# An opening in eight chunks of 256 channels instead of four of 512

## The chip, the cores and the metric

## What is computed

The kernel is one decoder layer on 256 tokens of 2048 channels. Only its beginning matters here:

```python
mod = c_act @ w_ada[l] + b_ada[l]                 # (2048,) @ (2048, 12288)
sh1, sc1, gt1, sh2, sc2, gt2 = split(mod, 6)
h = x * (1.0 + sc1) + sh1                         # x: 256 x 2048
proj = h @ w_in[l]
xr, gr, q_c, kv_c, k_r, g_rnn, g_mla = split(proj)
...   # recurrent branch, attention, output projection, norm, expert layer, norm
```

No row of `proj` can be finished before all 2048 channels of `h` are there, and a channel of `h` needs its column of `sh1` and of `sc1`, that is a sum over all 2048 rows of `w_ada`. The opening therefore reads the first 4096 columns of `w_ada` (32 MB), sums them on DVE, and multiplies the channels of `h` that are ready with the rows of `w_in` that belong to them.

## The kernel before

**Layout.** Channels lie on the 128 partitions in 16 tiles of 128 (`KT`), so `hT` is 16 tiles of 128 x 256 tokens. `x` is loaded transposed into the place of `hT` and changed there. `ring` is four slots of 1 MB (2048 words on each partition).

**The opening** goes over four chunks `j` of 512 channels (four tiles of `hT`). For each chunk:

1. SP (function `ada`, L378) loads eight ring slots of `ada_first`. One slot holds two of the 16 row tiles `kt`, each 1024 wide (512 columns of shift and 512 of scale). A slot is loaded again as soon as DVE has used both of its row tiles (semaphore `ada_used`). Behind the chunk's slots SP issues the early weights: a unit of 1 MB for each of three projections (`B_QC`, `B_KVC`, `B_XR`, L395) and half a unit (L398). In chunk 0 it also loads `xT` (2 MB, L389) and `w_kr` (1 MB, L400).
2. DVE adds the 16 row tiles up: one TENSOR_SCALAR (L1480) and 15 SCALAR_TENSOR_TENSOR (L1478), each 128x1024, each waiting for the one before by semaphore, since they all write the same sum. The sum is still spread over partitions.
3. PE (`ada_columns`) multiplies the sum, in eight pieces of 128 columns, by a column of ones. Each piece gives one column of shift or scale.
4. DVE adds the bias (L1486, L1487) and changes four tiles of `hT` by L1491 (semaphore `hT_ok`).
5. PE multiplies: `early_unit` three times (four tiles deep, four matmuls each), `w_kr` (four matmuls), then `ada_columns` of the next chunk, then `early_half` (eight matmuls). PE works in this order and cannot take the later one first.

Between the chunks DVE does small work that other parts need: `softplus()` after chunk 0 (L1412 to L1436), `angles()` after chunk 1 (L1441 to L1458), `sines()` after chunk 2. ACT answers with an exponential and two sines.

**Behind the opening** ACT copies the latents out of PSUM (L1059), `krraw` (L1064), the recurrent input (L1068) and its gate (L1072, which waits for the last `early_half`), DVE squares the latents, and PE goes on with norms, queries and the loop over heads. Weights for that loop are requested when the latents are normed, and POOL's loads of the rest of `w_ada` start after `rope_ok`.

Of the kernel before, what the change touches and what calls it, by code (L numbers as in the profile page):

```python
# [12 lines left out]
ALU = mybir.AluOpType  # L13
# [30 lines left out]
B_QC, B_KVC, B_XR, B_G, B_G2, B_RNN, B_MLA, B_O, B_WQ, B_END = 0, 1, 2, 10, 12, 18, 22, 26, 30, 34  # L44
ADA_UNITS = 2 * KT
SLOT_BASE = ADA_UNITS // RING - B_XR
B_SPLIT = B_XR + 2
# [42 lines left out]
def layouts(a):  # L90

    w_in, w_ada = a["w_in"][0], a["w_ada"][0]
    first = w_ada[:, :2 * D].reshape(2, RING, 2, P, 2, 4, 512).transpose(5, 0, 1, 3, 2, 4, 6)
    uq = a["w_uq"][0].reshape(LT, P, HEADS, NOPE + ROPE)
# [52 lines left out]
def build(nc, t, out):  # L147
    with ExitStack() as ctx:
        def sem(name):
            return ctx.enter_context(nc.semaphore(name))  # L150
# [16 lines left out]
        def at(off, n):  # L167
            return arena[:, off:off + n]
# [9 lines left out]
        def small(n):  # L178
            sm[0] += n
            assert sm[0] <= ARENA  # L180
            return sm[0] - n
# [5 lines left out]
        hT = at3(R_HT, KT, S)  # L187
        acc = at(R_G + KT * S, 2 * D).rearrange("p (j h c) -> p j h c", j=4, h=2)

# [14 lines left out]
        cact = at(small(16), 16)  # L204
        sh1 = at(small(4), 4)
        sc1 = at(small(4), 4)
        sp4 = at(small(16), 16)
# [112 lines left out]

        in_cst, in_par, in_pos, in_xT, in_kr = (sem(n) for n in ("in_cst", "in_par", "in_pos", "in_xT", "in_kr"))
        in_ring = [sem(f"in_ring{i}") for i in range(RING)]
        in_head = [sem(f"in_head{i}") for i in range(2)]
# [5 lines left out]
        in_early = [sem(f"in_early{i}") for i in range(6)]  # L329
        halves_used = sem("halves_used")  # L330
        in_ada = [sem(f"in_ada{i}") for i in range(3)]
# [39 lines left out]
        def _(sp):  # L371
            sp.dma_start(at(o_par, P + 24 + 6 * KT), t["par"]).then_inc(in_par, 16)

            def ada(j, i, first):
                for s in range(RING):
                    if not first:
                        sp.wait_ge(ada_used, i * 8 + (16 * j + 2 * (s - 3)))
                    sp.dma_start(ring[s], t["ada_first"][bass.ds(i * (RING * P) + (8 * j + s) * P, P), :]).then_inc(in_ring[s], 16)  # L378

# [5 lines left out]

            for j in range(4):
                if j == 0:
                    ada(0, 0, True)
                    sp.dma_start(at(R_HT, KT * S), t["xT"]).then_inc(in_xT, 16)  # L389
                with sp.Fori(1 if j == 0 else 0, 2) as i:  # L390
                    ada(j, i, False)
                for c, b in enumerate((B_QC, B_KVC, B_XR)):
                    if j >= 2:
                        sp.wait_ge(unit_used, 3 * j - 5 + c)
                    sp.dma_start(early_flat[3 * (j % 2) + c], input_unit(b, j)).then_inc(in_early[3 * (j % 2) + c], 16)  # L395
                if j >= 2:
                    sp.wait_ge(halves_used, j - 1)
                sp.dma_start(half_flat[j % 2], half_unit(0, j)).then_inc(in_head[j % 2], 16)  # L398
                if j == 0:
                    sp.dma_start(at(R_OT, KT * 2 * ROPE), t["w_kr"]).then_inc(in_kr, 16)  # L400

            def units(w, g, b):
# [5 lines left out]
            sp.dma_start(at(R_G, LT * HEADS * ROPE), t["w_uqr"]).then_inc(in_uqr, 16)  # L408
            sp.wait_ge(ada_used, 2 * ADA_UNITS)
            for s in range(RING):  # L410
# [56 lines left out]
            query_weights(9, in_wq[9])  # L467
            sp.wait_ge(modc_done, 12)
            query_weights(10, in_wq[10])
# [135 lines left out]
        def _(pe):  # L605
# [17 lines left out]
            def early_half(j):  # L623

                pe.wait_ge(in_head[j % 2], 16 * (j // 2 + 1))
                for k in range(4):
                    kt = 4 * j + k
                    for m in range(2):
                        last = mm(ps[:, 5, m * S:(m + 1) * S], half_w[j % 2][:, k, m * P:(m + 1) * P], hT[:, kt, :], kt == 0 and m == 0, kt == KT - 1)
                last.then_inc(halves_used, 1)  # L630

            def ada_columns(j):

                pe.wait_ge(acc_ok, j + 1)
                for h in range(2):
                    for k in range(4):
                        o = S + 8 * j + 4 * h + k
                        last = mm(ps[:, 4, o:o + 1], acc[:, j, h, k * P:(k + 1) * P], ones[:, 0:1], j == 0 and h == 0 and k == 0, True)
                last.then_inc(modc_done, 1)

            def early_unit(j, c):

                o = ps[:, (6, 2, 0)[c]:(6, 2, 0)[c] + 2, :].rearrange("p b (h c) -> p (b h) c", h=2)
                i = 3 * (j % 2) + c
                pe.wait_ge(in_early[i], 16 * (j // 2 + 1))
                for k in range(4):
                    kt = 4 * j + k
                    for m in range(4):
                        last = mm(o[:, m, :], early_w[i][:, k, m * P:(m + 1) * P], hT[:, kt, :], kt == 0 and m % 2 == 0, kt == KT - 1)
                last.then_inc(unit_used, 1)  # L650

            ada_columns(0)
            for j in range(4):
                pe.wait_ge(hT_ok, 4 * j + 4)
                for c in range(3 if j < 3 else 2):
                    early_unit(j, c)
                pe.wait_ge(in_kr, 16)
                for kt in range(4 * j, 4 * j + 4):
                    last = mm(ps[:, 4, 0:S], krw[:, kt, :], hT[:, kt, :], False, kt == KT - 1)
                if j < 3:  # L660
                    ada_columns(j + 1)
                    early_half(j)
            last.then_inc(kr_done, 1)
            early_unit(3, 2)
            early_half(3)
            pe.wait_ge(kr_out, 1)
# [28 lines left out]
            def queries(h):  # L695
                b = h % 2
                pe.wait_ge(in_head[b], 32 * (h // 2 + 2))
                if h and h % 4 == 0:
# [344 lines left out]
        def _(act):  # L1043
# [6 lines left out]
            A(sigc, colB[:, 0:16], ACT.Sigmoid).then_inc(sigc_ok, 1)  # L1050
            act.wait_ge(y_need, 1)
            A(lt[1], lt[0], ACT.Exp, scale=-1.0).then_inc(y_ok, 1)
            act.wait_ge(r_ok, 1)
            A(pt[3], pt[2], ACT.Sin).then_inc(sin_ok, 1)
            A(pt[4], pt[2], ACT.Sin, scale=0.5).then_inc(sin_ok, 1)

            def latent(b, off, bank):
# [12 lines left out]
            channels_out(B_XR, infront(XR, 1024))  # L1070
            act.wait_ge(halves_used, 4)
            A(infront(GR, 512), ps[:, 5, :], ACT.Copy)  # L1072
# [325 lines left out]
        def _(dve):  # L1398
# [69 lines left out]

            for j in range(4):
                part = at(R_G + KT * S + 1024 * j, 1024)  # L1470
                for kt in range(KT):
                    i, s = kt // 8, kt // 2 % RING
                    if kt % 2 == 0:
                        dve.wait_ge(in_ring[s], j * 32 + 16 * (i + 1))
                    raw = ring[s][:, kt % 2 * 1024:(kt % 2 + 1) * 1024]
                    if kt:
                        dve.wait_ge(ada_used, j * KT + kt)
                        STT(part, raw, cact[:, kt:kt + 1], part, ALU.mult, ALU.add).then_inc(ada_used, 1)  # L1478
                    else:
                        TS(part, raw, cact[:, 0:1], None, ALU.mult).then_inc(ada_used, 1)  # L1480
                dve.wait_ge(ada_used, j * KT + KT)
                dve.sem_inc(acc_ok, 1)

                dve.wait_ge(modc_done, j + 1)
                dve.wait_ge(in_xT, 16)
                me.do(TT(sh1, ps[:, 4, S + 8 * j:S + 8 * j + 4], modc[:, 4 * j:4 * j + 4], ALU.add))  # L1486
                me.do(TT(sc1, ps[:, 4, S + 8 * j + 4:S + 8 * j + 8], modc[:, KT + 4 * j:KT + 4 * j + 4], ALU.add))  # L1487
                me.wait()
                for k in range(4):
                    h = at(R_HT + 1024 * j + S * k, S)  # L1490
                    TS(h, h, sc1[:, k:k + 1], sh1[:, k:k + 1], ALU.mult, ALU.add).then_inc(hT_ok, 1)  # L1491
                if j == 0:
                    softplus()
                if j == 1:
                    angles()
                if j == 2:
                    sines()

            for i, lat in enumerate((qcT, kvT)):
# [104 lines left out]
            def columns(n, count):  # L1604
                dve.wait_ge(modc_done, 4 + n + count)
                c = modc[:, 2 * KT + 8 * n:2 * KT + 8 * (n + count)]
                TT(c, c, ps[:, 4, 0:8 * count], ALU.add).then_inc(col_ok, 1)
# [471 lines left out]
```

## Time and profile before

| | us |
|---|---|
| median of 3 runs | 2320.36 (2319.26 to 2324.15) |
| the profiled execution | 2321.49 |
| its span, first to last instruction | 2319.5 |
| PE busy / DVE busy in the span | 2058.7 (89%) / 1483.0 (64%) |
| bytes read | 805.10 MB |

All times of rows are counted from the start of the span. A timeline row gives start, length, engine, line, operation and how many of them it merges, with the idle time ahead of it and what ended that. The chain of work that ended last is followed back from the last instruction. A windows row gives the busy time of each engine in a stretch, with the clock granted to TensorE as a share of full speed, the busy share of the DMA engines and what they moved.

### The profile page before, as it was taken

How to read it: one execution, taken by the hardware profiler on the slowest of the kernel's cores; microseconds unless marked ns; L12 is line 12 of the kernel's file. 1: busy time of each engine (PE TensorE's matmuls, PEld its weight loads, DVE VectorE, ACT ScalarE, POOL GpSimd, SP SyncE). 2: the span in 40 equal slices, each digit the busy share in tenths (PEclk: the TensorE clock that was granted, in tenths of full speed). 3: DMA queues.
4: the chain of work that ended last, by engine and by line, in shares of the span. 5: the costliest groups of instructions: out<-in, count | busy, mean ns of one | idle time of the engine just before them, and what ended most of it. 6: DMA issues, size and time to landing. Idle time of an engine off the chain costs nothing.

```text
span 2319.5 us, 23058 instructions
## 1 busy us (share of the span) xinstructions
PE 2058.7 (89%) x7678; PEld 1334.9 (58%) x7678; DVE 1483.0 (64%) x2119; ACT 573.3 (25%) x1103; POOL 763.3 (33%) x764
## 2 busy tenths in 40 slices
PE   3999999999999999999987888787878788888977
PEld 3888999977888887787433333333333333333333
DVE  6837866967876556688366656664666668465444
ACT  0014455453343333322111101111111111112011
POOL 0001010101211000056465554555555454445562
PEclk9999999999999999999999888988898998889999
DMA  9946676657988664689899999999999999999996
GB/s 394 421 199 243 228 272 216 242 210 280 385 315 284 224 219 163 254 354 406 362 422 421 422 422 422 422 422 421 422 421 422 422 421 421 422 421 417 420 423 263
DMA packets 125637, 808.30 MB, mean 348 GB/s; under 512 B 14068, under 2 KB 14452, under 8 KB 38132
## 3 DMA queue, kind: packets, MB, share of 16 engines
q0 software_dynamic: 92160, 604.02, 63.9%
q1 hardware_dynamic: 33112, 202.70, 23.4%
q8 instruction: 51, 0.84, 0.1%
q10 hardware_dynamic: 288, 0.53, 0.1%
q14 instruction: 26, 0.21, 0.0%
HBM read 805.10 MB, written 2.10 MB: 348 GB/s over the span
## 4 chain that ended last, share of the span: by engine, by line
PE 53%; DMA 22%; DVE 8%; POOL 7%; issue 6%; ACT 4%; POOLq 0%; ACTq 0%; DVEq 0%; SPq 0%
PE ps L607 52%; DMA front<-in_peer_u,arena 17%; DVE front L1977 3%; DMA front<-in_ada_first 2%; POOL arena L548 2%; POOL front L540 1%; POOL arena L540 1%; POOL arena L528 1%; DMA front<-in_peer_v,arena 1%; DMA arena<-in_peer_v,arena 1%; DMA arena<-in_w_ada 1%; DVE arena L1478 1%; POOL front L548 1%; POOL front L594 0%; DVE split_ring L1631 0%
## 5 line engine op out<-in xcount | busy, mean ns | idle before, releaser
L607 PE MATMUL ps<-arena 128*128 128x512 f32 (+5 forms) x2798 | 962.4, 497 | 237.5 <-ACT arena L1297 186.9
L607 PEld LDWEIGHTS ps<-arena 128*128 128x128 f32 (+1 forms) x2798 | 512.7, 206 | 669.3 <-issue 486.0
L1977 DVE CUSTOM_DVE_ANT_0 front<-front,arena 128x2048 f32<-128x2048 f32 x180 | 410.0, 2293 | 201.2 <-DMA front<-in_peer_u,arena 195.0
L607 PE MATMUL ps<-front,arena 128*128 128x512 f32 (+1 forms) x832 | 355.9, 576 | 2.2 <-DMA front<-in_peer_v,arena 2.2
L1977 DVE CUSTOM_DVE_ANT_0 arena<-arena 128x2048 f32<-128x2048 f32 x60 | 137.4, 2294 | 265.6 <-DMA arena<-in_peer_u,arena 264.7
L607 PEld LDWEIGHTS ps<-front,arena 128*128 128x128 f32 x832 | 157.3, 190 | 191.3 <-issue 186.0
L540 POOL DMA_INDIRECT front<-in_peer_u,arena x176 | 239.0, 1358 | 68.4 <-issue 44.9
L1285 ACT ACTIVATE arena<-arena 128x4 f32<-128x4 f32 x64 | 13.2, 207 | 906.9 <-DVE arena L1957 906.7
L1631 DVE TENSOR_TENSOR split_ring<-front,split_pada 128x2048 fp32r<-128x2048 f32 x72 | 164.9, 2291 | 110.5 <-ACT split_pada L1180 110.1
L528 POOL COPY arena<-arena 128x4 uint32 (+1 forms) x120 | 85.8, 715 | 377.7 <-PE ps L607 356.9
L1180 ACT ACTIVATE split_pada<-front 128x2048 fp32r<-128x2048 f32 x70 | 134.1, 1916 | 234.4 <-PE ps L607 234.4
L499 POOL DMA_DIRECT2D arena<-in_w_ada x64 | 34.0, 532 | 474.3 <-DVEq L1543 189.2
L548 POOL DMA_INDIRECT arena<-in_peer_v,arena x153 | 162.1, 1060 | 77.7 <-POOL arena L528 48.6
L607 PE MATMUL ps<-arena,front 128*128 128x256 f32 (+2 forms) x864 | 173.0, 360 | 0.6 <-ACT arena L1311 0.6
L607 PEld LDWEIGHTS ps<-arena,front 128*128 128x128 f32 x864 | 152.6, 195 | 18.9 <-ACT arena L1311 0.8
L607 PE MATMUL ps<-split_pada,split_ht 128*128 128x512 f32 x320 | 125.8, 393 | 0.0
L607 PE MATMUL ps<-split_f,split_ring 128*128 128x256 f32 x384 | 108.6, 283 | 0.0
L504 POOL DMA_DIRECT2D arena<-in_w_ada x64 | 33.8, 528 | 210.8 <-DVE front L1727 103.6
L607 PE MATMUL ps<-split_pada,split_w 128*128 128x512 f32 x256 | 101.3, 396 | 1.8 <-DVE split_ring L1631 1.8
L607 PE MATMUL ps<-split_ring,split_f 128*128 128x512 f32 x256 | 101.3, 396 | 0.0
L607 PE MATMUL ps<-split_ring,split_w 128*128 128x512 f32 x256 | 100.4, 392 | 0.0
L548 POOL DMA_INDIRECT front<-in_peer_v,arena x91 | 90.0, 989 | 29.3 <-issue 29.3
(254 smaller groups left out, 2561.2 us busy)
## 6 DMA issues: line engine op xcount, KB each, us to landing
front<-in_w_in_u SPq DMA_DIRECT2D x64, 1024.0 KB, 6.8
arena<-in_w_ada POOLq DMA_DIRECT2D x128, 512.0 KB, 6.4
front<-in_ada_first SPq DMA_DIRECT2D x32, 1024.0 KB, 11.8
front<-in_w_rnn_out_u SPq DMA_DIRECT2D x16, 1024.0 KB, 6.3
front<-in_w_mla_out_u SPq DMA_DIRECT2D x16, 1024.0 KB, 4.9
front<-in_w_o_u SPq DMA_DIRECT2D x16, 1024.0 KB, 4.8
front<-in_peer_wq_u SPq DMA_DIRECT2D x11, 1024.0 KB, 8.8
arena<-in_w_ukv_h SPq DMA_DIRECT2D x16, 512.0 KB, 5.5
```

The costliest lines, as they stand in the source:

```text
L499: pool.dma_start(ada_raw[i % 3], ada_v[:, i % KT:i % KT + 1, 2 * D + 1024 * (i // KT):2 * D + 1024 * (i // KT + 1)].rearrange("p t c -> p ...
L504: pool.dma_start(ada_raw2[kt % 4], ada_v[:, kt:kt + 1, bass.ds(n * 1024 + 4 * D, 1024)].rearrange("p t c -> p (t c)")).then_inc(in_ada2[kt ...
L528: me.do(pool.tensor_copy(ix[:, e % 8:e % 8 + GROUP], arena[:, bass.ds(H * TOPK + (o_idx + e), GROUP)].bitcast(U32)))
L540: pool.indirect_dma_start(uslot[s], None, t["peer_u"][0], bass.IndirectOffsetOnAxis(idxu[:, s:s + 1], 0)).then_inc(in_u[s], 16)
L548: pool.indirect_dma_start(vslot[s], None, t["peer_v"][0], bass.IndirectOffsetOnAxis(idxv[:, s:s + 1], 0)).then_inc(in_v[s], 16)
L607: return pe.matmul(o, l, r, start=start, stop=stop, skip_group_check=True, **k)
L1180: A(whi[s % 2], ring[s], ACT.Copy).then_inc(whi_ok, 1)
L1285: me.do(A(zs[:, c0:c1], zu[:, c0:c1], ACT.Sigmoid, scale=GELU_S))
L1478: STT(part, raw, cact[:, kt:kt + 1], part, ALU.mult, ALU.add).then_inc(ada_used, 1)
L1631: TT(wlo[s], ring[s], whi[s % 2].bitcast(F32), ALU.subtract).then_inc(wlo_ok, 1)
L1977: V.tensor_tensor_reduce(uslot[s], uslot[s], h2[T], 1.0, 0.0, ALU.mult, ALU.add, zraw[:, s:s + 1]).then_inc(dots_done, 1)
```

## The change

The opening runs over `CHUNKS = 8` chunks of 256 channels (two tiles of `hT`). A ring slot still has 1 MB but now holds four row tiles, each 512 wide (256 of shift, 256 of scale), so a chunk takes four slots. DVE's sums are 128x512 and twice as many. `ada_columns` takes four pieces for a chunk, `hT` is changed two tiles at a time. The early weights come in half units: each of the old transfers is two of half the bytes, and `early_unit`, `early_half` and the `w_kr` products run two tiles deep. Of `xT` the first two tiles come ahead of the early weights (0.25 MB) and the other 14 behind `w_kr`. `softplus()` is now after chunk 5, `sines()` after chunk 3, `angles()` stays after chunk 1; ACT does the sines before the exponential.

```diff
-                    sp.dma_start(ring[s], t["ada_first"][bass.ds(i * (RING * P) + (8 * j + s) * P, P), :]).then_inc(in_ring[s], 16)
+                    if j:
+                        sp.wait_ge(ada_used, KT * (j - 1) + 4 * (s + 1))
+                    sp.dma_start(ring[s], t["ada_first"][(RING * j + s) * P:(RING * j + s + 1) * P, :]).then_inc(in_ring[s], 16)
...
+            for j in range(CHUNKS):
+                u, k = j // 2, j % 2
+                ada(j)
                 if j == 0:
-                    ada(0, 0, True)
-                    sp.dma_start(at(R_HT, KT * S), t["xT"]).then_inc(in_xT, 16)
-                with sp.Fori(1 if j == 0 else 0, 2) as i:
-                    ada(j, i, False)
+                    sp.dma_start(at(R_HT, 2 * S), t["xT"][:, 0:2 * S]).then_inc(in_xT0, 16)
...
+                    i, before = 3 * (u % 2) + c, 2 * (u // 2) + k
+                    if before:
+                        sp.wait_ge(in_early[i], 16 * before)
+                    sp.dma_start(early_flat[i][:, 1024 * k:1024 * (k + 1)], input_unit(b, u)[:, 1024 * k:1024 * (k + 1)]).then_inc(in_early[i], 16)
...
                 if j == 0:
                     sp.dma_start(at(R_OT, KT * 2 * ROPE), t["w_kr"]).then_inc(in_kr, 16)
+                    sp.dma_start(at(R_HT + 2 * S, (KT - 2) * S), t["xT"][:, 2 * S:]).then_inc(in_xT, 16)
...
-            for j in range(4):
-                part = at(R_G + KT * S + 1024 * j, 1024)
+            for j in range(CHUNKS):
+                part = at(R_G + KT * S + 512 * j, 512)
                 for kt in range(KT):
-                    i, s = kt // 8, kt // 2 % RING
-                    if kt % 2 == 0:
-                        dve.wait_ge(in_ring[s], j * 32 + 16 * (i + 1))
-                    raw = ring[s][:, kt % 2 * 1024:(kt % 2 + 1) * 1024]
+                    s = kt // 4
+                    if kt % 4 == 0:
+                        dve.wait_ge(in_ring[s], 16 * (j + 1))
+                    raw = ring[s][:, kt % 4 * 512:(kt % 4 + 1) * 512]
...
-                for k in range(4):
-                    h = at(R_HT + 1024 * j + S * k, S)
+                for k in range(2):
+                    h = at(R_HT + 512 * j + S * k, S)
                     TS(h, h, sc1[:, k:k + 1], sh1[:, k:k + 1], ALU.mult, ALU.add).then_inc(hT_ok, 1)
-                if j == 0:
-                    softplus()
                 if j == 1:
                     angles()
-                if j == 2:
+                if j == 3:
                     sines()
+                if j == 5:
+                    softplus()
```

## Rows read from the trace of the kernel before

**Rows 1.** The chain of work that ended last, stretch 0 to 260 us: start us, us, what.
```profile
10.76 12.66 DMA front<-in_ada_first
...
23.45 1.30 DVE arena L1478
...
24.77 1.30 DVE arena L1478
...
26.16 1.29 DVE arena L1478
...
66.64 150.79 PE ps L607 x754
```

**Rows 2.** Windows: length, busy time by engine, PEclk, DMA share, GB/s.
```profile
8.70:128.00 119.30, 89.09 (x412) 78.88 (x413) 92.36 (x116) 2.22 (x4) 0.00 (x0) 0.97 1.01 422
128.00:157.00 29.00, 29.00 (x136) 25.51 (x136) 3.35 (x5) 3.74 (x5) 0.00 (x0) 1.00 0.33 136
```

**Rows 3.** Timeline of the opening, SP's issues and the first sum.
```profile
8.66 0.75 DVE L1480 TENSOR_SCALAR arena<-front,arena 128x1024 f32<-128x1024 f32 x1 [3.58 <-DMA front<-in_ada_first]
...
10.76 8.72 SPq L378 DMA_DIRECT2D front<-in_ada_first  x4
```

**Rows 4.** Timeline, DVE: what stands between two chunks.
```profile
37.96 0.16 DVE L1486 TENSOR_TENSOR arena<-ps,arena 128x4 f32<-128x4 f32 x1 [3.79 <-PE ps L607]
...
38.23 1.38 DVE L1491 TENSOR_SCALAR arena<-arena 128x256 f32<-128x256 f32 x4
39.53 0.17 DVE L1412 TENSOR_SCALAR arena<-arena 128x16 f32<-128x16 f32 x1
...
43.55 0.18 DVE L1436 TENSOR_SCALAR arena<-arena 128x16 f32<-128x16 f32 x1
...
70.25 0.16 DVE L1486 TENSOR_TENSOR arena<-ps,arena 128x4 f32<-128x4 f32 x1 [3.72 <-PE ps L607]
...
75.01 0.75 DVE L1480 TENSOR_SCALAR arena<-front,arena 128x1024 f32<-128x1024 f32 x1 [0.16 <-DVE arena L1458]
75.80 20.30 DVE L1478 SCALAR_TENSOR_TENSOR arena<-front,arena 128x1024 f32<-128x1024 f32 x15
```

**Rows 5.** Timeline, PE: columns of a chunk (128x1) and the products (128x256).
```profile
34.38 3.55 PE L607 MATMUL ps<-arena 128*128 128x1 f32 x16 [34.38 <-DVEq L1482]
...
116.74 7.07 PE L607 MATMUL ps<-arena,front 128*128 128x256 f32 x32
```

**Rows 6.** Windows around the columns of chunks 1 and 3.
```profile
38.00:39.60 1.60, 0.00 (x0) 0.00 (x0) 1.56 (x7) 0.00 (x0) 0.00 (x0) 1.00 1.07 435
...
63.80:66.10 2.30, 0.05 (x1) 0.00 (x0) 2.16 (x3) 0.00 (x0) 0.00 (x0) 1.00 0.98 410
66.10:72.90 6.80, 6.26 (x23) 5.72 (x24) 2.93 (x11) 0.00 (x0) 0.00 (x0) 0.53 1.02 422
...
125.40:127.20 1.80, 1.80 (x18) 1.80 (x17) 0.00 (x0) 0.00 (x0) 0.00 (x0) 1.00 1.07 441
```

**Rows 7.** Groups by line and form, DVE: count, busy us, mean ns, idle before.
```profile
L1478 DVE SCALAR_TENSOR_TENSOR arena<-front,arena 128x1024 f32<-128x1024 f32 x60 | 77.1, 1284 | 9.7 <-DMA front<-in_ada_first 6.1
...
L1987 DVE SCALAR_TENSOR_TENSOR arena<-arena 128x512 f32<-128x512 f32 x8 | 6.0, 748 | 0.1
...
L1513 DVE SCALAR_TENSOR_TENSOR arena<-arena 128x256 f32<-128x256 f32 x8 | 3.3, 481 | 0.1
...
L1864 DVE TENSOR_SCALAR arena<-arena 128x512 f32<-128x512 f32 x4 | 1.9, 546 | 0.0
```

**Rows 8.** Timeline, the end of the opening.
```profile
127.25 0.16 DVE L1486 TENSOR_TENSOR arena<-ps,arena 128x4 f32<-128x4 f32 x1 [2.54 <-PE ps L607]
...
156.72 0.60 ACT L1072 ACTIVATE front<-ps 128x512 f32<-128x512 f32 x1 [2.43 <-PE ps L607]
```

**Rows 9.** DMA issues, whole span: count, KB each, median us from issue to landing.
```profile
front<-in_w_mla_out_u SPq DMA_DIRECT2D x16, 1024.0 KB, 4.9
...
arena<-in_w_uq_h SPq DMA_DIRECT2D x16, 256.0 KB, 3.3
```

## What the change does to the time, and why

> **What bounds the kernel now.** I read the chain of work that ended last first, because it says which engine the opening waits for. Up to 66.6 us it alternates between transfers of `ada_first` and DVE's sums; from 66.64 us it is PE without a gap for 150.8 us [rows 1]. So the kernel ends when PE's row of work ends, and two things about PE matter: when it can start, and how much stands behind the last sum. The windows say the same: between 8.7 and 128 us the DMA engines are full at 422 GB/s, PE is busy 89.1 of 119.3 us and DVE 92.4; between 128 and 157 us PE is busy for all 29 us and hardly anything else runs [rows 2]. PE's first instruction is at 34.38 us [rows 5], since the first sum needs 8 MB.
>
> The marker for everything below is ACT's copy at 156.72 us, which waits for the last product of the opening [rows 8]. What follows has no clock of its own: the head loop's weights wait for the normed latents, and POOL's loads wait for the ropes. Hence I let a shift of the marker pass to the end one for one.
>
> **What the change gives: a shorter tail.** Before, the columns of the last chunk are done at 127.2 us [rows 6]. Then come 16 instructions of a half, 96 of three units, 8 of `w_kr` and 16 of the last half: 136 instructions in 29.5 us [rows 6, 8], 0.217 us each, which is the count of the busy window too [rows 2]. After it, a chunk has half of everything: 8 + 48 + 4 + 8 = 68 instructions, 14.75 us. The gain is **14.8 us**, if the columns of the last chunk were done at the same time.
>
> **What it costs: DVE's sums.** They are not halved by halving their width. The same operation with a per-partition scalar takes 481 ns at 256 wide, 748 at 512 and 1284 at 1024 [rows 7]: 1.04 to 1.05 ns an element and some 210 ns that each instruction has anyway. From start to start there are 1.32 us, or 1.39 where a ring slot is waited for too [rows 1], so 0.04 and 0.11 above the duration. One chunk is then one TENSOR_SCALAR of about 0.48 (546 ns for the 512-wide form with two scalars, which is the upper bound; 0.75 at 1024 [rows 3, 7]), 15 sums of 0.748, 15 steps of 0.04 and three ring waits of 0.07: **12.5 us** (12.4 to 12.6). Eight chunks are 100 us, where four took 21.1 us each (75.01 to 96.10 [rows 4]), 84 us. That is 16 us more work on DVE.
>
> **Between two chunks** DVE waits for PE's columns. Today that is 3.79 us for 16 instructions that take PE 3.55 [rows 4, 5], so 0.24 us of handing over. Eight instructions take 1.8 us at this pace; at the pace of chunk 3, 16 in 1.8 us [rows 6], they take 0.9. The bias and the first change of `hT` follow at +0.27, and with two tiles instead of four (1.38 us for four [rows 4]) DVE is free at about +0.95. A gap is thus 2.1 us with PE at full clock and 3.0 with PE at half clock. There are eight of them instead of four.
>
> **Beside the chunks** stand 4.2 us of `softplus` (39.53 to 43.73) and 3.1 of `angles` (70.25 to 75.01 less the 1.65 of bias and `hT`) [rows 4], and some 1.0 of `sines` (three operations of 256 wide, none above 0.48 [rows 7]). Today PE's queue covers them; the sums are ready before PE asks. If DVE is the bound they cost their full 8.3 us. Moving `softplus` behind chunk 5 takes it out of the stretch in which DVE waits for transfers anyway.
>
> **The supply.** Transfers are served in the order of their issue. The slot issued at 10.76 us arrives 12.66 us later [rows 1, 3]: since the first slot came in at 8.6, six MB were ahead of it or in it (three slots, `xT`, itself), 6.29 million bytes in 14.8 us, 424 GB/s, the full rate [rows 2]. In the new order there are between the first slot's arrival and the first slot of chunk 1: three slots, 0.25 MB of `xT`, 1.75 of early weights, 1 of `w_kr`, 1.75 of `xT` and the slot itself, 8.75 MB are 9.17 million bytes, 21.6 us. It arrives at **30.2 us**, while DVE is free at 24.2: a stall of 6 us. From then a chunk needs 5.75 MB, 14.2 us of transfer, against 14.6 us of DVE; slots are asked for 3 us apart and arrive 2.5 us apart. By the same count the first slot of chunk 2 arrives at 44.5 us and DVE wants it at 48.8, that of chunk 3 at 58.8 against 63.4. So from chunk 2 on I take no stall.
>
> At this place a rule speaks against the change. The Trainium skill, DMA: Bandwidth & Descriptors, section "Anatomy of one DMA", gives each transfer a fixed cost of about 2 us beside its bytes, and its section on bandwidth asks for 1 MB or more. The full stretch above shows that this cost overlaps when transfers queue; it is the last rival below.
>
> **The sum, in times of the trace.** Chunk 0 is summed from 8.66 to 21.2 us, `hT` ready 24.2 (PE starts at half pace as today). Chunk 1: 30.2 to 42.7, ready 45.7 (PE idle before, half pace), `angles` to 48.8. Chunk 2: to 61.3, ready 63.4. Chunk 3: to 75.9, ready 78.0, `sines` to 79.0. Chunk 4: to 91.5, ready 93.6. Chunk 5: to 106.1, ready 108.2, `softplus` with ACT's exponential to 112.4. Chunk 6: to 124.9. Is PE in time? Behind the columns it has a half (1.7) and then units and `w_kr` (11.3), 13.0 us, while the next sum is done 13.7 us behind them: PE idles 0.7 us a chunk, but 5 us ahead of chunk 6. There the clock falls. Today an idle time of 2.3 to 2.8 us before chunk 1 is followed by 6.8 us at 0.53 of full clock, the lower of the two levels (1.2 and 2.4 GHz), while 1.6 us at 38 to 39.6 left the record at 1.00 [rows 6]. 6.8 us at half clock lose 3.4 us of PE's work. So the columns of chunk 6 end at 126.8, `hT` is ready at 127.9, the sum of chunk 7 ends at 140.4; PE reaches its columns at 126.8 + 13.0 + 1.7 (half of the loss; the other part falls into the idle time and the columns) = 141.5 and ends them at 142.4. With the tail of 14.75 the marker is at 157.2, against 156.72: +0.5 us.
>
> Two things that no row prices: the half units arrive in pieces of half the length, and a wait of SP for an earlier landing stands in front of each second half. SP's wait holds only transfers that are asked for a chunk ahead. The shorter pieces can lengthen the stall before chunk 1, by nothing up to 2 us; I take 0.5, near the row at full rate. In all **+1.0 us**: 2322.5 against the profiled 2321.49, and 2321.4 against the median, which lies 1.1 below that execution. Put in words, the last columns are done 15.2 us later than today (142.4 against 127.2), although PE starts 13 us earlier, and that eats the 14.8 us of shorter tail.
>
> **The rivals.**
> - *The clock falls in more chunks (slower).* PE has only 0.7 us of slack a chunk, and `angles` and `sines` widen two idle times to about 1.5 to 3.8 us. Each further dip costs 0.9 us in the columns and most of the other 2.5 in the products. It decides from an idle time between 1.6 us (no fall) and 2.8 us (fall) [rows 6]. The Trainium skill, TensorE: Matmul & The Clock Gate, "HAM oscillation", tells of such a saw-tooth; the row at 0.53 agrees that idle time is followed by half clock. Two or three dips more, the last of them in the tail where nothing covers it, give +6 to +9 us: 2328. Against it: PE that is late has no idle time, so dips do not follow one another. Chance 0.22.
> - *The supply is better than the order of issue (faster).* If the slots of chunk 1 come beside the early weights and not behind them, the stall of 6 us goes and with it all that follows: -5 us, 2315.5. The 12.66 us of today's slot speak against it. Chance 0.12.
> - *DVE is quicker than I count (faster).* If sum and gap were 0.7 us a chunk shorter, PE's 13.9 us of work would be the bound, -4 to -5 us, 2316. The 512-wide row speaks against it. Chance 0.08.
> - *The shift does not reach the end*, because something in the head loop is late anyway. The chain is PE's through 217 us [rows 1], so hardly; it gives 2320.4. Chance 0.05.
> - *Small transfers bound the opening (slower).* A lone transfer of 1 MB takes 4.9 us and one of 0.25 MB 3.3 [rows 9], so 2.8 us do not depend on size. Were these paid one after another, 17 more transfers cost 48 us: 2368. Today's 1 MB each 2.5 us contradict it. Chance 0.03.
> - The forecast itself has 0.50, from 2318 to 2325.
>
> **Numbers.** A measurement can tell 0.2%, 4.6 us, from no change. Faster by more: most of the two faster rivals, 0.17. Slower by more: the clock rival, the last one and the upper edge of the forecast, 0.29. Same: 0.54. The range reaches over the faster rivals and the clock rival, 2314.5 to 2329.5, and leaves out the last one and the far ends.
>
> **What would show it.** Right: DVE's sums at about 0.75 us and x120 of them; the first sum of chunk 1 waiting for a transfer at 24 to 30 us; from chunk 2 DVE without waits for transfers and PE waiting for DVE; DMA below full rate from about 80 us; the clock at half around 125 us; the marker at 157. Wrong: PE without gaps (then DVE is not the bound), sums waiting for slots beyond chunk 1 (then the supply is), or half clock in more than three chunks.

## The result, and the profile after

The changed kernel takes 2324.20 us in the median of 20 runs (2322.66 to 2327.89), the one before 2320.66 (20 runs, 2317.99 to 2324.34). The ratio is **1.0014** (95% interval 1.0008 to 1.0020), so the change costs 3.2 us by the ratio and 3.5 by the medians, under the 0.2% that counts as a difference here. 2321.4 was forecast, with 2314.5 to 2329.5 as the range: the time lies in it, 2.8 us above the forecast. All ratios here are of fast executions alone, which leaves out one execution of 5524 us of the first experiment. The profiled execution took 2323.56 us, with a span of 2321.9 instead of 2319.5.

Timeline of the changed kernel, DVE and PE in the opening (start us, us, engine, line, operation, what ended the idle time before it). L1489 are the sums, L1491 the first of a sum, L1503 the change of `hT`:

```profile
9.23 11.98 DVE L1489 SCALAR_TENSOR_TENSOR arena<-front,arena 128x512 f32<-128x512 f32 x15
...
21.41 1.83 PE L614 MATMUL ps<-arena 128*128 128x1 f32 x8 [21.41 <-DVEq L1493]
...
23.55 0.73 DVE L1503 TENSOR_SCALAR arena<-arena 128x256 f32<-128x256 f32 x2
...
31.30 0.49 DVE L1491 TENSOR_SCALAR arena<-front,arena 128x512 f32<-128x512 f32 x1 [7.02 <-DMA front<-in_ada_first]
...
49.93 0.49 DVE L1491 TENSOR_SCALAR arena<-front,arena 128x512 f32<-128x512 f32 x1 [0.16 <-DVE arena L1469]
...
62.55 1.05 PE L614 MATMUL ps<-arena 128*128 128x1 f32 x8 [2.30 <-DVEq L1493]
...
109.27 0.17 DVE L1423 TENSOR_SCALAR arena<-arena 128x16 f32<-128x16 f32 x1
...
113.50 0.49 DVE L1491 TENSOR_SCALAR arena<-front,arena 128x512 f32<-128x512 f32 x1
...
126.12 1.87 PE L614 MATMUL ps<-arena 128*128 128x1 f32 x8 [4.75 <-DVEq L1493]
...
127.85 15.29 PE L614 MATMUL ps<-arena,front 128*128 128x256 f32 x56
...
144.82 0.16 DVE L1498 TENSOR_TENSOR arena<-ps,arena 128x2 f32<-128x2 f32 x1 [3.39 <-PE ps L614]
...
159.61 0.60 ACT L1083 ACTIVATE front<-ps 128x512 f32<-128x512 f32 x1 [0.70 <-PE ps L614]
```

PE starts at 21.4 instead of 34.4 us [rows 5]. But between chunk 1 and the end it no longer works without a gap: the idle times before the columns (2.30, 4.75 us) end with DVE's queue (`DVEq`), so PE waits for sums. The marker, 156.72 us before [rows 8], is at 159.61. Of the chain that ended last, PE's unbroken piece began at 66.64 us [rows 1]; now it is this:

```profile
11.58 19.70 DMA front<-in_ada_first
31.30 0.50 DVE arena L1491
31.83 0.76 DVE arena L1489
...
126.12 94.20 PE ps L614 x474
```

The chain runs over one transfer, then over DVE's sums one by one, and reaches PE for good 59.5 us later. DVE has taken PE's place as the bound. Only before the change of `hT` in the last chunk does DVE wait longer for PE (3.39 us, where a wait after columns at full clock is 1.2): there PE was late, by the clock. Two group rows answer to [rows 7]:

```profile
L1489 DVE SCALAR_TENSOR_TENSOR arena<-front,arena 128x512 f32<-128x512 f32 x120 | 90.2, 752 | 5.9
...
L1491 DVE TENSOR_SCALAR arena<-front,arena 128x512 f32<-128x512 f32 x8 | 3.9, 483 | 10.3 <-DMA front<-in_ada_first 10.1 <-DVE arena L1469 0.2
```

60 sums of 1284 ns, 77.1 us, became 120 of 752 ns, 90.2 us, and the only long wait for a transfer is the one at the start. Windows of the changed kernel (length, busy time of PE, PEld, DVE, ACT, POOL, PEclk, DMA share, GB/s) show the supply easing off and where the clock fell:

```profile
8.70:31.30 22.60, 8.80 (x32) 7.66 (x33) 12.72 (x20) 0.00 (x0) 0.00 (x0) 1.00 1.00 416
31.30:80.00 48.70, 39.61 (x183) 34.18 (x182) 41.51 (x71) 2.01 (x3) 0.00 (x0) 0.93 1.01 404
80.00:130.00 50.00, 43.37 (x202) 37.60 (x201) 42.27 (x82) 0.22 (x1) 0.00 (x0) 0.94 0.99 381
...
123.60:133.80 10.20, 7.68 (x22) 6.51 (x23) 7.76 (x15) 0.00 (x0) 0.00 (x0) 0.50 1.00 343
```

381 to 416 GB/s in place of 422 [rows 2], and 10.2 us at half clock in the middle of the last chunks. The 0.93 of the second row is another stretch, from 41.7 to 48.5 us, around the columns of chunk 1.

### The profile page after: what moved, and what is told of

It reads as the page before. It is cut to its first block, busy times and chain, and to the rows that moved or that the text cites. A ratio compares the mean times of both kernels' runs of the same rounds, so it can differ in the third digit from the quotient of the medians.

```text
span 2321.9 us, 23075 instructions
## 1 busy us (share of the span) xinstructions
PE 2069.4 (89%) x7678; PEld 1342.1 (58%) x7678; DVE 1498.4 (65%) x2191; ACT 572.9 (25%) x1103; POOL 749.4 (32%) x764
## 4 chain that ended last, share of the span: by engine, by line
PE 52%; DMA 19%; DVE 12%; POOL 6%; issue 6%; ACT 4%; POOLq 0%; DVEq 0%; ACTq 0%; SPq 0%
PE ps L614 52%; DMA front<-in_peer_u,arena 16%; DVE front L1989 4%; DVE arena L1489 3%; POOL arena L555 2%; POOL arena L547 1%; DMA front<-in_ada_first 1%; POOL front L547 1%; DMA front<-in_peer_v,arena 1%; DMA arena<-in_peer_v,arena 1%; POOL arena L535 1%; POOL front L555 1%; POOL front L601 0%; DVE arena L1896 0%; DVE arena L1899 0%
## 5 line engine op out<-in xcount | busy, mean ns | idle before, releaser
L547 POOL DMA_INDIRECT front<-in_peer_u,arena x176 | 233.0, 1324 | 68.3 <-issue 44.9
L535 POOL COPY arena<-arena 128x4 uint32 (+1 forms) x120 | 77.0, 642 | 392.9 <-PE ps L614 369.6
```

The costliest lines, as they stand in the source:

```text
L535: me.do(pool.tensor_copy(ix[:, e % 8:e % 8 + GROUP], arena[:, bass.ds(H * TOPK + (o_idx + e), GROUP)].bitcast(U32)))
L547: pool.indirect_dma_start(uslot[s], None, t["peer_u"][0], bass.IndirectOffsetOnAxis(idxu[:, s:s + 1], 0)).then_inc(in_u[s], 16)
```

## Experiments

Theory: from chunk 1 on DVE's chain (sum, columns, change of `hT`) sets the time; it stands still for 7.0 us at 24.3 to 31.3 us for lack of a slot; small functions on DVE cost their length outside that gap and nothing inside it; and PE's clock, which by this theory falls behind idle time, adds 1 to 3 us. Rivals: PE's own work is the bound; the supply or its smaller transfers are. "The marker" is ACT's copy behind the opening's last product (L1072 before, L1083 after, shifted by lines in edited kernels).

| run | marker us | ratio to the kernel before (95%) |
|---|---|---|
| before | 156.72 | 1 |
| changed | 159.61 | 1.0014 (1.0008 to 1.0020) |
| changed, a second profile | 161.84 | one execution, 2324.6 us |
| softplus behind chunk 0 | 154.23 | 0.9985 (0.9974 to 0.9996) |
| softplus and angles behind chunk 0 | 152.81 | 0.9979 (0.9969 to 0.9988) |
| the same, PE kept busy | 152.00 | 0.9981 (0.9973 to 0.9990) |
| changed, PE kept busy in one gap | 158.44 | 1.0012 (1.0003 to 1.0021) |
| changed, half the sums narrow | 144.77 | 0.9945 (0.9930 to 0.9960) |
| changed, `w_kr` and `xT` later | 159.66 | 1.0001 (0.9992 to 1.0010) |
| `w_kr`, `xT` later, small functions behind chunk 1 | 154.80 | 0.9974 (0.9964 to 0.9983) |
| before, transfers split | 157.81 | 1.0007 (0.9998 to 1.0017) |
| before, softplus behind chunk 2 | 157.46 | 1.0014 (1.0005 to 1.0023) |

### Softplus back in the gap

```diff
-                if j == 5:
-                    softplus()
+                if j == 0:
+                    softplus()
```
(ACT's exponential ahead of its sines again.)

> The changed kernel with softplus behind chunk 0 again instead of behind chunk 5, and ACT's exponential ahead of the sines. My theory: DVE is the bound from chunk 1 on, but stands still for 7.0 us at 24.3 to 31.3 us, waiting for a slot. There the 4.2 us of softplus cost nothing. The first sum of chunk 1 stays at 31.3 us, the sum of chunk 6 starts at 109.3 instead of 113.5 us, PE idles 0.5 us before it instead of 4.75, so its clock doesn't fall, and the columns of chunk 7 are no longer late. The marker (ACT's copy behind the last product, 159.61 us in the changed kernel, 156.72 in the one before) comes to 152.1 us: 7.5 us less than the changed kernel, some 4 us less than the kernel before (ratio to before 0.998). Rival, the place of softplus doesn't matter because PE's work is the bound: marker within 1 us of 159.6, ratio 1.001.

The ratio is 0.9985, against 1.0014 for the changed kernel: 6.7 us less by the ratios (by their intervals 4 to 10; 5.4 by the markers), and less than the kernel before too. Timeline, DVE and PE:

```profile
31.34 0.49 DVE L1491 TENSOR_SCALAR arena<-front,arena 128x512 f32<-128x512 f32 x1 [3.02 <-DMA front<-in_ada_first]
...
111.12 0.48 DVE L1491 TENSOR_SCALAR arena<-front,arena 128x512 f32<-128x512 f32 x1
...
123.74 1.05 PE L614 MATMUL ps<-arena 128*128 128x1 f32 x8 [0.52 <-DVEq L1493]
...
154.23 0.60 ACT L1083 ACTIVATE front<-ps 128x512 f32<-128x512 f32 x1 [0.70 <-PE ps L614]
```

The first sum of chunk 1 starts where it did, the wait before it is 3.02 instead of 7.02 us: softplus is hidden. PE's idle time before the columns of chunk 6 is 0.52 us and they run at full pace. The marker is 2.1 us above what was expected, and the windows say why:

```profile
62.50:64.60 2.10, 2.02 (x13) 1.92 (x14) 0.90 (x5) 0.00 (x0) 0.00 (x0) 1.00 0.99 351
64.60:68.00 3.40, 3.40 (x10) 2.67 (x9) 3.18 (x6) 0.00 (x0) 0.00 (x0) 0.52 0.97 382
...
95.30:98.70 3.40, 3.40 (x10) 2.75 (x9) 3.18 (x7) 0.00 (x0) 0.00 (x0) 0.52 0.93 341
```

Two stretches of 3.4 us at half clock, behind idle times of only 1.05 and 1.36 us and the columns that followed them. Each loses 1.7 us of PE's work; PE has 0.7 us of slack, and the change of `hT` behind it comes 0.94 us late. So the gain has two parts: 2.4 us until the sum of chunk 6 (111.12 against 113.50), which is softplus less the two falls, and 3.0 us behind it, where the clock no longer falls.

### Both small functions in the gap

```diff
                 if j == 0:
                     softplus()
+                    angles()
-                if j == 1:
-                    angles()
```
(against the run above)

> The changed kernel with softplus and angles both behind chunk 0, in the 7.0 us in which DVE waits for the first slot of chunk 1 (ACT's exponential ahead of the sines). My theory: of the 4.2 + 3.1 us 7.0 are hidden there. The sum of chunk 1 starts at 31.4 to 31.7 us, that of chunk 2 at 46.9 instead of 49.9, just when its slot comes (with narrow sums the slots of chunks 3 and 4 were there at 61.3 and 75.7 us, 14.4 apart; DVE needs 14.6). Marker 3 us below that of the run with softplus alone moved (154.23 there, with two half-clock stretches of 3.4 us in its profile that cost 0.9 us each): 150 to 152 us, ratio to before 0.997. Rival, the supply is the bound from there on: the sums of chunks 2 to 4 wait for slots by more than 1 us each and the marker stays above 153.

Ratio 0.9979, marker 152.81, 0.8 above the expected range, with half clock twice, from 41.8 and from 93.0 us. The sum of chunk 1 starts at 31.94, half a microsecond behind `angles`, that of chunk 2 at 47.4. The stretch from 41.8 us took 10.2 us, and PE's products of chunk 1 ran so late by it that `hT` of chunk 2 was changed 3.5 us after its sum ended (63.41 against 59.9) and not 1.5 (63.90 against 62.44 in the changed kernel). No sum of chunks 2 to 4 waited for a slot, so the rival of the supply is out. By its intervals this run isn't told apart from the one above; both beat the changed kernel.

### What the fallen clock costs

```diff
+                if j == 5:
+                    for n in range(12):
+                        mm(ps[:, 4, S + 64:2 * S], krw[:, 0, :], hT[:, 0, 0:192], False, True)
                 if not end:
                     ada_columns(j + 1)
```

> The changed kernel with 12 added matmuls (24 instructions, 192 wide, into a part of a PSUM bank that nobody reads) on PE behind the products of chunk 5, where PE would idle 4.75 us while DVE does softplus and the sum of chunk 6. They take about 3.9 us and end before the sum does. It tells apart what the fallen clock costs. My theory: no half clock at 124 to 134 us; the 56 products that took 15.3 us from 127.85 us take 12.3; columns of chunk 6 take 1.0 instead of 1.9; DVE's sum of chunk 7 ends at 140.6, the marker comes to 156.4 us, 3.2 less than the changed kernel, ratio to before 1.000. Rival, the clock is not what delayed the end (the sums alone are the bound): marker at 158.7 to 159.6, ratio 1.001.

Windows of this run around the gap:

```profile
121.40:128.00 6.60, 5.75 (x34) 5.25 (x32) 6.03 (x9) 0.00 (x0) 0.00 (x0) 1.00 0.95 331
128.00:134.00 6.00, 6.00 (x32) 5.41 (x33) 4.66 (x10) 0.00 (x0) 0.00 (x0) 1.00 0.94 349
```

The clock stays up there, and the way from the start of chunk 6's columns to the marker is 30.5 us (127.96 to 158.44) instead of 33.5 (126.12 to 159.61): 3 us, where 3.2 were expected. But the columns of chunk 6 themselves came 1.8 us later, because this execution had two stretches at half clock, from 64.0 and from 94.7 us, that the first profile of the changed kernel lacks. The marker, 158.44, is thus just below the rival's range and 2 us above the theory's. The ratio, 1.0012, is not to be told from 1.0014. So the price of the one stretch is shown in one pair of traces, and no gain in the timed runs; in the second profile of the changed kernel (next) the same place costs only 1.4 us.

### Is it the same in every execution?

> The changed kernel once more, one look. It asks whether the stretches at half clock are the same in every execution. In the first profile there were two, at 41.7 to 48.5 and 123.6 to 133.8 us, and none at 64 and 95 us, where the runs with changes only elsewhere had one each behind idle times of 1.0 to 1.4 us of PE. Theory: the two behind idle times of over 4 us come again, those behind 1.0 to 1.4 us come or don't; each that comes delays the sums behind it by 0.9 us, and the marker lies between 159.6 and 161.5 us. Rival, they are fixed by the program: the same two stretches and 159.6 us within 0.2.

```profile
62.81 1.87 PE L614 MATMUL ps<-arena 128*128 128x1 f32 x8 [2.10 <-DVEq L1493]
...
95.48 1.05 PE L614 MATMUL ps<-arena 128*128 128x1 f32 x8 [1.37 <-DVEq L1493]
...
131.60 13.77 PE L614 MATMUL ps<-arena,front 128*128 128x256 f32 x56
...
161.84 0.60 ACT L1083 ACTIVATE front<-ps 128x512 f32<-128x512 f32 x1 [0.70 <-PE ps L614]
```

No. The same kernel now has half clock four times before 140 us (from 42.4, 62.8, 97.0 and 127.7 us). The columns of chunk 2 take 1.87 us at 62.81, where they took 1.05 at 62.55, behind the same 2.1 to 2.3 us of idle time; 1.37 us before 95.48 are followed by a fall, the same 1.37 before 92.65 in the first profile are not. The marker is 2.2 us later, a little above the range expected. Idle times of 1.4 to 2.3 us are thus followed by half clock in some executions of this kernel and not in others. And the fall before the last chunk, which came both times behind 4.75 us of idle time, began later here (127.7 instead of 123.6 us): the 56 products took 13.77 us instead of 15.29, a loss of 1.4 and not 3.0 against the 12.33 that they take at full clock.

### PE kept busy everywhere

The second of the better kernels, with added matmuls:

```diff
+                for n in range(0 if end else 16 if j == 0 else 1):
+                    mm(ps[:, 4, S + 64:2 * S], krw[:, 0, :], hT[:, 0, 0:192], False, True)
```

> The run with both small functions behind chunk 0, and on PE added matmuls that nobody reads, between the products of a chunk and the wait for the next sum: 16 (5.2 us) in chunk 0, one (0.3 us) in each of chunks 1 to 6. They fill most of PE's idle time. Theory, short idle times of about 1 us before the columns are enough to let the clock fall in some executions: then this profile has no half-clock stretch from 45 to 150 us (or one less than its neighbours have), columns of chunk 1 take 1.0 instead of 1.9 us, and the marker comes 1 to 3 us below that of the run without them. Rival, the one-column matmuls of the columns themselves, not the idle time, let the clock fall: the stretches at half clock stay, and only the columns of chunk 1 gain 0.9 us.

```profile
92.26 1.05 PE L614 MATMUL ps<-arena 128*128 128x1 f32 x8 [1.05 <-DVEq L1495]
...
44.70:51.50 6.80, 6.80 (x20) 5.81 (x21) 4.71 (x10) 0.00 (x0) 0.00 (x0) 0.50 1.01 423
51.50:151.00 99.50, 97.71 (x474) 85.53 (x474) 75.36 (x120) 3.05 (x4) 0.00 (x0) 1.00 0.92 366
```

Full clock for 99.5 us, with the one-column matmuls unchanged and idle times before them of 0.2 us, once 1.05. The run without the added matmuls had one stretch in this time, so this is one less, as the theory has it; but falls come in some executions and not in others, and one profile is no proof. The filling of chunk 0 was too short (2.02 us of idle time were left, and one stretch at half clock came). The marker gains 0.8 us, less than the 1 to 3 expected; the ratio, 0.9981 against 0.9979, shows nothing.

The rival, that the one-column matmuls let the clock fall, is not out, and another profile speaks for it, that of the kernel before with softplus behind chunk 2 (last experiment). Two windows and a row of PE's timeline:

```profile
80.00:99.30 19.30, 19.21 (x97) 16.82 (x96) 16.43 (x17) 0.00 (x0) 0.00 (x0) 1.00 1.01 420
99.30:102.70 3.40, 3.40 (x10) 2.71 (x9) 2.79 (x14) 0.22 (x1) 0.00 (x0) 0.51 1.02 423
...
98.02 5.39 PE L607 MATMUL ps<-arena,front 128*128 128x256 f32 x16
```

PE was busy for 19.21 of 19.3 us, the last 1.9 of them before the products with the 16 one-column instructions of chunk 2, and then the clock was at half for 3.4 us; the 16 products took 5.39 us, where they take 3.70 in the kernel before, whose clock stayed up at this place. So idle time isn't needed for a fall. What decides between the executions stays open.

### What is behind DVE

```diff
-                        STT(part, raw, cact[:, kt:kt + 1], part, ALU.mult, ALU.add).then_inc(ada_used, 1)
+                        n = 16 if kt % 2 else 512
+                        STT(part[:, 0:n], raw[:, 0:n], cact[:, kt:kt + 1], part[:, 0:n], ALU.mult, ALU.add).then_inc(ada_used, 1)
```

> The changed kernel with every second row tile summed over 16 columns instead of 512 (the rest of these sums is left out of the computation; all transfers, waits and products stay). A chunk costs DVE 7.9 instead of 12.5 us. It takes DVE out as the bound and shows what is behind it. My theory: then the supply and PE are the bound, 14.2 and 13.9 us a chunk: the last slot arrives at about 126 us, the columns of chunk 7 end at about 131 and the marker stands at 146 us, 13 to 14 us less than the changed kernel, with DMA full until 130 us; ratio to before 0.996. Rival, PE's own order with its fallen clock is the bound already: marker no lower than 156 us.

This kernel leaves out 496 of the 512 columns of every second row tile. Ratio 0.9945; marker 144.77 us, 14.8 below the changed kernel, a little more than the 13 to 14 expected (behind 47 us its profile has no half clock, either). DVE waits for a slot at nearly every fourth sum:

```profile
61.26 0.49 DVE L1492 TENSOR_SCALAR arena<-front,arena 128x512 f32<-128x512 f32 x1 [1.41 <-DMA front<-in_ada_first]
...
66.22 2.08 DVE L1490 SCALAR_TENSOR_TENSOR arena<-front,arena 128x512 f32<-128x512 f32 x4 [0.39 <-DMA front<-in_ada_first]
68.70 2.08 DVE L1490 SCALAR_TENSOR_TENSOR arena<-front,arena 128x512 f32<-128x512 f32 x4 [0.41 <-DMA front<-in_ada_first]
75.70 0.48 DVE L1492 TENSOR_SCALAR arena<-front,arena 128x512 f32<-128x512 f32 x1 [1.15 <-DMA front<-in_ada_first]
```

Chunks follow one another at 14.4 us, the time of 5.75 MB, where the sum was 14.2. Against the kernel before, eight chunks with a quick DVE gain 12.0 us at the marker and 12.8 by the ratio; with the full sums DVE takes all of that away and 3 us more. PE has the same work as in the changed kernel, so this also throws out the rival that PE is the bound.

### The arithmetic of the supply

```diff
                 ada(j)
+                if j == 1:
+                    sp.dma_start(at(R_OT, KT * 2 * ROPE), t["w_kr"]).then_inc(in_kr, 16)
+                    sp.dma_start(at(R_HT + 2 * S, (KT - 2) * S), t["xT"][:, 2 * S:]).then_inc(in_xT, 16)
...
-                if j == 0:
-                    sp.dma_start(at(R_OT, KT * 2 * ROPE), t["w_kr"]).then_inc(in_kr, 16)
-                    sp.dma_start(at(R_HT + 2 * S, (KT - 2) * S), t["xT"][:, 2 * S:]).then_inc(in_xT, 16)
```

Both transfers now stand behind the slots of chunk 1 and ahead of its early weights.

> The changed kernel with the key weights (w_kr, 1 MB) and the rest of xT (1.75 MB) issued behind the slots of chunk 1 instead of ahead of them. It tests the arithmetic of the supply: 2.75 MB less stand ahead of the first slot of chunk 1, 6.8 us at 424 GB/s. My theory: the sum of chunk 1 starts at 24.5 to 25 us instead of 31.3; the first slot of chunk 2 then comes at 46 to 47 us as before, since the bytes ahead of it are the same, so DVE waits there, angles is hidden in that wait, and the sum of chunk 2 starts at 46 to 47 instead of 49.9. Marker 3 us less than the changed kernel (156.6, with 1 us either way by the clock), ratio to before 1.000. Rival, all 6.8 us are kept to the end: marker 152.8. Rival, transfers are not served in the order of issue: the sum of chunk 1 stays after 29 us.

```profile
25.01 0.49 DVE L1491 TENSOR_SCALAR arena<-front,arena 128x512 f32<-128x512 f32 x1 [0.74 <-DMA front<-in_ada_first]
...
46.70 0.49 DVE L1491 TENSOR_SCALAR arena<-front,arena 128x512 f32<-128x512 f32 x1 [3.44 <-DMA front<-in_ada_first]
...
59.32 1.86 PE L614 MATMUL ps<-arena 128*128 128x1 f32 x8 [7.22 <-DVEq L1493]
```

Both arrivals are as worked out: 25.0 and 46.7 us. Transfers are served in their order, and what the first chunk wins the second waits for. Yet the marker is at 159.66, not 156.6. PE idled 7.22 us before the columns of chunk 2, its clock was at 0.50 from 55.5 to 65.7 us, and again from 93.0 and 123.7. The sum of chunk 2 is 3.2 us earlier than in the changed kernel, that of chunk 3 2.4, those of chunks 4 and 5 0.9, that of chunk 6 not at all: each loss stands behind one of the first two of these stretches. The ratio, 1.0001, is 0.0013 below that of the changed kernel, at the edge of what the intervals tell.

Both ideas together, `w_kr` and `xT` later and both small functions behind chunk 1:

> The changed kernel with w_kr and the rest of xT behind the slots of chunk 1, and softplus and angles both behind chunk 1. It joins the two ways of using the stall and tells whether they add up. My theory: they don't, both end at the arrival of the first slot of chunk 2. The sum of chunk 1 starts at 25.0, the one of chunk 2 at 46.7 to 47.8 us (it was 47.4 with the small functions behind chunk 0), marker 151 to 154, ratio to before 0.998. Rival, they add up: the sum of chunk 2 starts at 41 to 44 us, marker 147 to 150, ratio 0.996.

The ratio is 0.9974, the lowest of the kernels that compute everything, though its interval overlaps with those of the others in the group. The sum of chunk 2 started at 49.09 us, later than either theory said, since that of chunk 1 began at 26.43 instead of 25.0 and the 7.3 us of small work now stood in DVE's chain with no wait left to hide in. The change of `hT` in chunk 1 also waited 0.6 us beyond PE for `xT`:

```profile
40.75 0.16 DVE L1498 TENSOR_TENSOR arena<-ps,arena 128x2 f32<-128x2 f32 x1 [1.82 <-DMA arena<-in_xT]
...
49.09 0.49 DVE L1491 TENSOR_SCALAR arena<-front,arena 128x512 f32<-128x512 f32 x1 [0.16 <-DVE arena L1469]
```

So the two ways don't add up, and the marker, 154.80, is 0.8 above the range, with half clock three times (from 41, 57.8 and 95.3 us, 10.2 us long from 57.8). That its time is nonetheless no worse than with the small functions behind chunk 0, where the marker was 2.0 us earlier, stays open; single profiles differ by that much.

### The price of the smaller transfers, alone

```diff
-                    sp.dma_start(early_flat[3 * (j % 2) + c], input_unit(b, j)).then_inc(in_early[3 * (j % 2) + c], 16)
+                    for k in range(2):
+                        cs = slice(1024 * k, 1024 * (k + 1))
+                        sp.dma_start(early_flat[3 * (j % 2) + c][:, cs], input_unit(b, j)[:, cs]).then_inc(in_early[3 * (j % 2) + c], 16)
```
(and the half units alike)

> The kernel before, with each early transfer (units of 1 MB, halves of 0.5 MB) issued as two of half the bytes and half the row length; nothing else. It measures by itself what 16 more and shorter transfers cost. My theory: transfers queue behind one another and the fixed part overlaps, so the full stretch still moves 410 to 422 GB/s; the shorter rows may cost up to 2 us over the whole opening, and PE's queue covers most of it: marker 156.7 to 158 us, ratio 1.000 to 1.0005. Rival, each transfer has a fixed cost that is paid one after another (2.8 us): 45 us more, ratio 1.019.

Ratio 1.0007 (0.9998 to 1.0017), no difference shown. From 8.6 to 125 us the run moved 414 GB/s where the kernel before moved 421 and the next run, with whole transfers, 419. The rate was low in two stretches, 88 to 97 and 116 to 125 us (378 and 380 GB/s, against 421 and 422 before). The second step of the last chunk's sum started at 105.69 instead of 104.15 us, the marker stands 1.1 us later. So in this profile the shorter pieces cost 1.5 us up to there, and no fixed 2.8 us each: that would be 45 us. The Trainium skill, DMA: Bandwidth & Descriptors, section "Anatomy of one DMA", attributes most of the fixed 2 us to waiting for the receipt of the last byte. It says this of transfers that GpSimd issues, while these are SP's; whatever the fixed part of SP's transfers is, it overlaps in a full queue here.

### A small function where PE is the bound

```diff
                 if j == 2:
                     sines()
+                    softplus()
```
(in the kernel before; the call behind chunk 0 is gone, ACT's exponential stands behind its sines)

> The kernel before with softplus behind sines after chunk 2 instead of behind chunk 0, ACT's exponential last. It asks what a small function costs on DVE where PE is the bound. My theory: the sum of chunk 3 ends at 127.5 to 128 us instead of 124.7, while PE is ready for its columns at 125.4; the marker moves by 2 to 2.6 us, less than the 4.2 us of work; ratio 1.001. Rival, PE's queue covers all of it: marker unmoved (156.7). Rival, all of it counts, as in the changed kernel: marker +4.2.

```profile
105.64 20.26 DVE L1478 SCALAR_TENSOR_TENSOR arena<-front,arena 128x1024 f32<-128x1024 f32 x15
126.01 1.95 PE L607 MATMUL ps<-arena 128*128 128x1 f32 x16 [0.16 <-DVEq L1482]
```

The sum ended at 125.9 us, earlier than the 127.5 expected. In the profile PE waited only 0.16 us for it, for it was late itself (half clock from 68.6 and 99.3 us), and the marker moved by 0.7 us. In the timed runs the ratio is 1.0014, 3.2 us with an interval of 1.2 to 5.3, which excludes only that nothing is moved; both the theory's 2 to 2.6 and the rival's 4.2 lie in it. How much of the 4.2 us PE's queue covers stays open.

## Why the prediction was right, and what it got wrong

| step | forecast | measured |
|---|---|---|
| a sum of 16 row tiles | 12.5 us | 12.50 (8.71 to 21.21) |
| 512-wide sum | 748 ns | 752 ns |
| gap between chunks, full / half clock | 2.1 / 3.0 us | 2.1 / 2.9 (62.44 to 64.55, 126.01 to 128.94) |
| softplus / angles in the chain | 4.2 / 3.1 us | 4.2 / 3.2 |
| first slot of chunk 1, without / with the 0.5 for shorter pieces | 30.2 / 30.7 us | 31.3 |
| half clock ahead of chunk 6 | 6.8 us, 1.7 lost beyond the idle time | 10.2 us, 3.0 lost |
| last columns done | 142.4 us | 144.8 |
| tail | 14.75 us | 14.8 |
| marker, without / with these 0.5 | 157.2 / 157.7 us | 159.6 |

**Right.** The forecast rested on two rows, the 512-wide operation with a scalar from memory and the order of the transfers, and both held: the sums to 1%, the order in the run that changed it, where both arrivals lay in the bounds given ahead. That DVE becomes the bound, that nothing waits for slots beyond chunk 1, and that the shorter tail is eaten by later last columns was seen as written. The shift of the marker, 2.9 us, is that of the span, 2.4, and of the medians, 3.5, within what executions differ by. The time alone would confirm little: the range is 15 us wide, four of the five rivals lie in it with their times (2315.5, 2316, 2320.4, 2328), and a change of +1.0 us was forecast where +3.2 came. It is the rows above that tell the forecast from the rivals.

**Mis-sized: the supply.** The first slot of chunk 1 came at 31.3, 1.1 us behind the count and 0.6 behind the count with its allowance. The step "the shorter pieces can lengthen the stall by nothing up to 2 us; I take 0.5" took too little: 416 GB/s instead of 424 to 31.3 us, and 1.5 us by 105.7 us in the run that split the transfers alone. Hardly any of that run's split transfers fall into the time up to 31.3 us (it moved 424 GB/s there), so what slowed this first stretch in the changed kernel is not shown by itself.

**Mis-sized by 1.3 us in this profile, and partly wrong: the clock.** The 56 products behind chunk 6's columns took 15.29 us where the same 56 behind chunk 2's took 12.33, a loss of 3.0 and not 1.7; in the second profile it was 1.4, so the size hangs on the execution. The threshold was wrong: "it decides from an idle time between 1.6 us (no fall) and 2.8 us (fall)". The row at 38.0 to 39.6 us reads 1.00 [rows 6], but the columns before it took 3.55 us [rows 5] where the same number at full clock takes 1.8 [rows 6], so the 1.00 cannot be right. In all runs here the first columns have the slow pace under a PEclk of 1.00; the value says nothing this early. Where it does, falls follow idle times of 1.05 and 1.37 us, and one came with PE never idle for more than 0.1 us. So the clock rival, given 0.22, was a part of what happened: it did not add its 6 to 9 us, but the two profiles of the changed kernel show two and four falls, at some 0.9 us each where PE's slack is short and 1.4 to 3 before the last chunk.

**Not foreseen: the gap as a place.** The text counted the stall of 6 us and the 8.3 us of small work in the same sum, and did not say that one could lie in the other. It even named the place, "moving `softplus` behind chunk 5 takes it out of the stretch in which DVE waits for transfers anyway", and read it the wrong way round: in that stretch softplus costs nothing. That was worth more than the change itself: moving softplus back gives 6.7 us by the ratios, with the fall of the clock that it spares, and the change costs 3.2.

## What to carry over

Halving the pieces of a pipeline halves its tail but not the fixed part of each instruction: with 210 ns of 1284 that does not depend on width, eight chunks cost DVE 16 us to save 14.8. Before cutting pieces smaller, lay out every engine's chain in times, find which engine the cut makes the bound, and see where that engine waits for data. Small work on it belongs into that wait, not behind it: moved there, the same eight chunks run 0.15 to 0.21% faster than the kernel before instead of 0.14% slower (0.26% with two transfers moved too).

## What the runs showed of the hardware

- Half clock on TensorE (0.50 to 0.53 of 2.4 GHz) came in stretches of 3.4, 6.8 and 10.2 us, and not in every execution of the same kernel. Idle times as short as 1.05 us, with eight one-column instructions behind them, stood before some; before one there was no idle time above 0.1 us, but 16 one-column instructions. The Trainium skill, TensorE: Matmul & The Clock Gate, "HAM oscillation", warns of idle gaps too, but only of longer ones; the falls behind 1.05 and 1.37 us here do not fit that, and the measurement decides. With most of PE's idle time filled there was none for 99.5 us, in one profile.
- Halving the length of rows and transfers of the early weights (14 MB of some 50) went with 414 GB/s over 116 us instead of 419 to 421, in one profile.
